# Hybrid trunk: z's SiLU ahead of the last two decays, earlier output gating, group sums between two weight blocks

## The reference, cut to what matters

```python
z, xbc, dt_raw, gate_b, x_b = jnp.split(hn @ hyb_w_in[j], HYB_SPLITS, axis=-1)
y_a = ssd_mixer(...)      # state-space heads, 16 heads of 64 channels
y_b = rglru_mixer(...)    # gated linear recurrence, 1024 channels
h = h + jnp.concatenate([y_a, y_b], axis=-1) @ hyb_w_out[j]

# inside ssd_mixer
y = ssd_chunked(xa, dt, a, bm, cm)            # per head: (C B^T * decay) @ x
y = y + d_skip[:, None] * xa
yg = (y * jax.nn.silu(z)).reshape(bsz, l, 2, 512)
yg = rms_norm(yg, norm_w.reshape(2, 512))     # root mean square over each group of 512 channels
```

## Time and profile before

| | us |
|---|---|
| median of the three runs | 1044.61 |
| the profiled execution, device time | 1044.93 |
| its span, first to last instruction | 1043.1 |
| TensorE matmul busy | 1033.4 (99%) |
| VectorE busy | 798.7 (77%) |
| ScalarE busy | 618.4 (59%) |
| TensorE clock granted, mean | 0.998 of full |
| 16 DMA engines, queue of the weight loads | 64.1% |

### The profile page before, as it was taken

The page is one execution under the profiler, slowest core; times in us unless marked ns, Lnnn a source line. Parts: engine busy times, 40 slices in busy tenths (PEclk is TensorE's granted clock), DMA queues, the critical chain, the costliest instruction groups (busy, mean ns, idle before and its releaser), DMA issues.

```text
span 1043.1 us, 18313 instructions
## 1 busy us (share of the span) xinstructions
PE 1033.4 (99%) x6526; PEld 931.3 (89%) x6526; DVE 798.7 (77%) x1226; ACT 618.4 (59%) x979; POOL 51.0 (5%) x70
## 2 busy tenths in 40 slices
PE   9999999999999999999999999999999999999997
PEld 7888888999999988888888888888998998888886
DVE  6888777789868888887766888776689578887763
ACT  7655555478878775565435566544467766556541
POOL 0200002100000000000111000011100000000021
PEclk9999999999999999999999999999999999999999
DMA  8866766559545666666865666676565456667671
GB/s 252 222 196 188 223 183 192 159 142 276 153 111 158 173 197 191 192 190 191 221 173 160 187 196 196 196 204 174 162 172 168 122 157 200 190 191 205 184 205 41
DMA packets 363299, 190.13 MB, mean 182 GB/s; under 512 B 6080, under 2 KB 360672, under 8 KB 363248
## 3 DMA queue, kind: packets, MB, share of 16 engines
q1 hardware_dynamic: 362848, 188.79, 64.1%
q0 software_dynamic: 256, 0.59, 0.3%
q10 hardware_dynamic: 144, 0.10, 0.1%
HBM read 187.86 MB, written 1.07 MB: 181 GB/s over the span
## 4 chain that ended last, share of the span: by engine, by line
PE 93%; DVE 3%; ACT 2%; issue 1%; SPq 1%; DMA 1%; DVEq 0%; ACTq 0%
PE psum L269 44%; PE psum L278 23%; PE psum L239 6%; PE psum L243 6%; PE psum L240 6%; PE psum L1834 1%; PE psum L254 1%; PE psum L1839 1%; PE psum L257 1%; PE psum L1763 1%; ACT whi L223 1%; DMA raw<-in_ffn_gate 1%; SPq L193 0%; DVE wlo L228 0%; PE psum L1123 0%
## 5 line engine op out<-in xcount | busy, mean ns | idle before, releaser
L228 DVE TENSOR_TENSOR wlo<-raw,whi 128x1024 fp32r<-128x1024 f32 (+1 forms) x322 | 415.3, 1307 | 68.9 <-ACT whi L223 67.4
L223 ACT ACTIVATE whi<-raw 128x1024 fp32r<-128x1024 f32 (+1 forms) x322 | 352.2, 1112 | 23.9 <-PE psum L243 19.3
L269 PE MATMUL psum<-xn,whi 128*128 128x512 f32 x1328 | 317.4, 391 | 0.0
L269 PEld LDWEIGHTS psum<-xn,whi 128*128 128x128 f32 x1328 | 244.3, 188 | 47.4
L278 PEld LDWEIGHTS psum<-xn,wlo 128*128 128x128 f32 x1328 | 170.3, 191 | 6.5
L278 PE MATMUL psum<-xn,wlo 128*128 128x256 f32 x1328 | 172.3, 283 | 0.0
L269 PE MATMUL psum<-hid,whi 128*128 128x512 f32 x704 | 166.5, 390 | 0.0
L269 PEld LDWEIGHTS psum<-hid,whi 128*128 128x128 f32 x704 | 129.9, 188 | 25.7
L239 PE MATMUL psum<-xn,whi 128*128 128x256 f32 x416 | 104.4, 289 | 0.0
L240 PE MATMUL psum<-xn,whi 128*128 128x256 f32 x416 | 101.9, 283 | 0.0
L636 ACT ACTIVATE arena<-arena 128x256 f32<-128x256 f32 x88 | 36.8, 418 | 107.2 <-DVE arena L713 107.2
(11 more groups left out here) (251 smaller groups left out, 979.6 us busy)
## 6 DMA issues: line engine op xcount, KB each, us to landing
raw<-in_ffn_down SPq DMA_DIRECT2D x64, 704.0 KB, 4.6
raw<-in_ffn_gate SPq DMA_DIRECT2D x87, 512.0 KB, 3.9
raw<-in_ffn_up SPq DMA_DIRECT2D x87, 512.0 KB, 4.0
raw<-in_hyb_w_in SPq DMA_DIRECT2D x36, 512.0 KB, 4.8
raw<-in_dif_w_qkv SPq DMA_DIRECT2D x24, 512.0 KB, 4.3
raw<-in_hyb_w_out SPq DMA_DIRECT2D x16, 512.0 KB, 4.8
raw<-in_dif_w_o SPq DMA_DIRECT2D x8, 512.0 KB, 3.9
hid<-cs_rows SPq DMA_DIRECT2D x4, 512.0 KB, 6.9
```

The source lines that it names most:

```text
L223: act.activation(whi[:, s, 0:k * P], raw[:, s, 0:k * P], ACT.Copy).then_inc(s_whi, 1)
L228: dve.tensor_tensor(wlo[:, s, 0:k * P], raw[:, s, 0:k * P], whi[:, s, 0:k * P].bitcast(F32), ALU.subtract).then_inc(s_wlo, 1)
L269: mm = pe.matmul(acc, tile_of(whi, s, k)[:, j, :], x[:, k0 + j, :, :], start=opens and j == 0, stop=closes and rest is not None and j == k ...
```

## The change

It changes lists of steps and no operation. On ScalarE both halves of SiLU(z) move from step 15 to step 14, ahead of the decays 6 and 7, which now both stand in step 14; the second four gates of the recurrence move from step 14 to step 15; the high parts of pairs 16 and 17 are no longer cut up by SiLU and squares. On VectorE the first three `gate_y` move to step 15, ahead of the products of decays 6 and 7; `lru_ix(1)` moves behind `read_pair(14)`; `take_y(6)`, `take_y(7)` and `gate_y(3)` move from step 17 to the end of step 16. On TensorE the group sums move from after pair 16 to between its two blocks.

```diff
-            after[16] += [group_sums]
+            middle[16] += [group_sums]
...
-            for m in range(8):
+            for m in range(6):
                 todo[8 + m] += [lambda m=m: decay(m)]
...
-            todo[14] += [lambda t=t: gates(t) for t in range(4, 8)]
-            todo[15] += [lambda: convert_hi_half(16, 0), lambda: silu_z(0), lambda: silu_z(1), lambda: convert_hi_half(16, 1)]
+            todo[14] += [lambda: silu_z(0), lambda: silu_z(1), lambda: decay(6), lambda: decay(7)]
+            todo[15] += [lambda t=t: gates(t) for t in range(4, 8)]
+            todo[15] += [lambda: convert_hi_half(16, 0), lambda: convert_hi_half(16, 1)]
             todo[16] += [lambda: square_y(0), lambda: square_y(1), lambda: square_y(2)]
-            todo[16] += [lambda: convert_hi_half(17, 0), lambda: square_y(3), lambda: convert_hi_half(17, 1)]
+            todo[16] += [lambda: square_y(3), lambda: convert_hi_half(17, 0), lambda: convert_hi_half(17, 1)]
...
-            for m in range(8):
+            for m in range(6):
                 first_work[9 + m] += [lambda m=m: decay_products(m)]
-            for m in range(8):
+            for m in range(6):
                 first_work[11 + m - m % 2] += [lambda m=m: take_y(m)]
...
-            todo[15] += [lambda: lru_ix(1)]
-            first_work[16] += [lambda: convert_lo_half(16, 0)] + [lambda k=k: gate_y(k) for k in range(3)]
-            first_work[16] += [lambda: convert_lo_half(16, 1)]
-            first_work[17] += [lambda: gate_y(3)]
+            first_work[15] += [lambda k=k: gate_y(k) for k in range(3)]
+            first_work[15] += [lambda: decay_products(6), lambda: decay_products(7)]
+            first_work[16] += [lambda: lru_ix(1), lambda: convert_lo_half(16, 0), lambda: convert_lo_half(16, 1)]
+            first_work[16] += [lambda: take_y(6), lambda: take_y(7), lambda: gate_y(3)]
```

## The result

The changed kernel takes 1045.87 us in the median of 19 runs (1045.61 to 1047.88), the kernel before 1044.47 us in 19 runs beside them (1043.74 to 1045.49). The ratio is 1.0016 with a 95% interval of 1.0011 to 1.0022: slower by 1.4 us, and within the 0.2% that was called no change. The forecast was 1046.2 us and +1.6 us.

A forecast was written before the change was run, and what follows sets the result against it. TensorE, 99% busy, was taken to bound the kernel, standing still 1.63 us at the output projection. A read 1.58 us later gave 1044.61 + 1.58 = 1046.2 us, other terms nothing; own range 1045.3 to 1047.0, full range 1044.5 to 1047.6.

The forecast's parts named there:

- The read holds the chain: VectorE's read of pair 16 waits for the block moved behind the sums, starting at 317.29 instead of 315.71, 1.58 us later.
- The stall: TensorE's wait for the last `y_lo` at the output projection grows from 1.63 to 3.21 us.
- The first output pair: Block 36 at the output projection: high part 0.25 us late, low part 1.1 us late in all, neither adding time.
- margin at block 30: ScalarE ahead of pair 15: high part of block 30 ready at 299.35, wanted at 300.45, 1.1 us of margin, no cost.
- Rival 2: Pair 15 starves behind ScalarE's SiLU, decays and extra loads: block 30 1.46 us late, 1047.6 us; chance 0.12.
- VectorE ahead of pair 16: VectorE's gates, products, low parts and last squares are done by 310.4, before the sums at 310.77; no cost.
- the start of the sum: The time of the kernel before from which the forecast counts: 1044.61 us.
- Rival 1: VectorE's first transpose starts on the root at about 314.2, the whole output projection stall goes: 1043.0 us; chance 0.06.
- Rival 3: The output projection stall comes from something both orders share, so the change does nothing: 1044.6 us; chance 0.06.

The follow-up runs named there:

- The first experiment: Changed kernel with VectorE's read of pair 16 moved behind the norm of tiles 0 to 3 and the second reciprocal: 1042.60 us, ratio 0.9984.
- the fourth: Kernel before with only the group sums moved between the two blocks of pair 16: 1046.59 us, ratio 1.0025.
- the copies: Changed kernel with four or eight small ScalarE copies ahead of the high part of block 30: 1046.69 us and 1049.59 us.
- fillers: 13 unread matmuls put into block 36's second-part waits, in the changed kernel (1045.75 us) and the kernel before with only the group sums moved (1046.37 us).

## Why the prediction was right

- **The read holds the chain.** Forecast: the read starts at 317.29, 1.58 us later than before. Measured on the same scale: 317.29. The first experiment takes this wait away and the loss with it; in the fourth the moved sums bring it back with nothing else changed.
- **The stall.** Forecast 3.21 us, measured 3.18. Tile 7 forecast at 329.55, measured 328.65 + 0.87 = 329.52.
- **The first output pair.** Forecast 0.25 us late for the high part and 1.1 in all for the low part, adding nothing to the end. Measured 0.29 and 0.29 + 0.80; the later wait shrank by as much, since its end is the last `y_lo`. That they don't add is shown by the total.
- **ScalarE.** Forecast margin at block 30 1.1 us; the trace of after gives 1.28 by records and the copies 1.1. Rival 2 needed ScalarE to take at least 1.1 us more than it did. The load costs 1.28 us and the engine starts it at once (284.82 to 284.83, 293.56 to 293.58), as forecast. What the Trainium skill's page ScalarE: Activation LUTs adds in What ACT_TABLE_LOAD costs, a drain at every switch, doesn't show here: the ACTIVATE behind the load at 293.58 starts 1.30 us after it.
- **VectorE ahead of pair 16.** Forecast: the last squares are over by 310.4, ahead of the sums at 310.77. Measured on the scale of before: 308.75 + 0.63 + 0.87 = 310.25. Nothing waits for it; the sums take 3.27 us from start to the next matmul, as before.
- **Size.** Both traces differ by 1.54 to 1.55 us behind the stall, the medians by 1.40. Both lie in the interval (1.1 to 2.3 us). Of the 0.3 us by which 1046.2 lies over the measured 1045.87, 0.14 come from the start of the sum, a median of three runs that 19 runs put lower (1044.47); the rest is within the scatter of the runs. The spans differ by 0.8 us only, since the profiled execution of before lost 0.87 us at its start; the forecast for the profiled execution, 1044.7, missed by that.
- **The rivals.** Rival 1 was the change as it would be with the read out of the way: its 1043.0 us stand beside 1042.6 and 1042.5 measured. Rival 2's sign did not come: pair 15 starts at 299.58 + 0.87 = 300.45, as before. Rival 3's did not either: the second part's low-part matmuls start at 328.99 + 0.87 = 329.86, where it had 328.32 and the forecast 329.9, and the interval of the ratio leaves out 1. The upper end of the range, set by rival 2, was not needed: the median lies inside the forecast's own 1045.3 to 1047.0. The low clock of three single runs, up to 1047.88 us, stood in no term of the sum; it left the median alone.

## What to carry to other kernels

When a step is moved ahead of another piece of work, ask what in the strict queues waits for the work that it overtakes: here the sums came 2.9 us earlier and the block that they overtook ended 3.4 us later, and a read of that block stood in front of the sums' only user. Before a gain is believed, follow the result through each engine's own order up to its first reader, row by row; by the traces one misplaced row turned a gain of 1.6 us into a loss of 1.5. Move the reader along with the producer, and not without it: the same edit of the read alone cost 0.6 us.

## What was not expected of the hardware

Behind a stall made of short waits TensorE's granted clock fell to its lower level. In the kernel with the sums alone the engine stood still, by starts, 0.4 us at the sums and then 3.2 us in pieces between 323.2 and 330.2; behind it the timeline has

```profile
330.19 0.89 PE L243 MATMUL psum<-hid,wlo 128*128 128x256 f32 x4
330.88 0.41 PE L239 MATMUL psum<-hid,whi 128*128 128x256 f32 x1
...
331.31 0.41 PE L239 MATMUL psum<-hid,whi 128*128 128x256 f32 x1
...
331.73 0.41 PE L239 MATMUL psum<-hid,whi 128*128 128x256 f32 x1
...
333.84 0.28 PE L239 MATMUL psum<-hid,whi 128*128 128x256 f32 x1
```

From one to the next it is 0.43 us where the same pair of matmuls takes 0.24 at the full clock, until 333.6. The 18 matmuls from 330.19 to 333.84 take 3.65 us instead of 18 x 0.12 = 2.16: the lapse costs 1.5 us. That run took 1048.18 us, the runs of the same kernel at a mean clock of 0.998 took 1046.21 to 1046.59, so it comes in some runs and not in others. The Trainium skill (TensorE: Matmul & The Clock Gate, HAM oscillation) tells of TensorE being set back to half its clock when it waits for a DMA between bursts of matmuls. The trace agrees in the level, 0.43 against 0.24 us; but the waits here were for VectorE and ScalarE, with matmuls between them, and none was longer than 0.8 us by starts.

Over all kernels a mean clock of 0.996 or less goes with a long stall. It came in none of 22 runs without a stall (the changed kernel with the read moved, in both places), none of 11 with 1.4 us, none of 68 of the kernel before (1.6 us), one of 11 with 2.2 us, 3 of 19 of the changed kernel (3.2 us), 3 of 7 with the sums alone (3.6 us), 3 of 11 with the copies, and none of 22 with fillers. That is what the runs show; which part of a stall decides it is not shown, and only one low run has a trace. Not every long run is of this kind: of the 87 runs of the kernel before one took 1046.69 us at a mean clock of 0.998, and the rest end at 1045.69.
